# Attention steps of a hybrid decoder kernel: the second half of the keys' logits goes between the turnings of two groups of blocks

## The reference, cut to what matters

```python
score = jnp.where(causal[None], score, -jnp.inf)
_, idx = lax.top_k(score, topk)
...
logits = jnp.einsum('bthd,btkhd->bthk', qb, k_sel).astype(jnp.float32) * dh ** -0.5
logits = logits + jnp.moveaxis(bias, -1, -2)
logits = jnp.where(valid[:, :, None, :], logits, -jnp.inf)
p = jax.nn.softmax(logits, axis=-1).astype(v.dtype)
return jnp.einsum('bthk,btkhd->bthd', p, v_sel)
```

## Time and profile before

| | us |
|---|---|
| median of 3 runs | 990.1 |
| lowest and highest | 987.07 and 993.2 |
| the profiled execution's own time | 989.08 |
| its span, first to last instruction | 987.0 |
| PE busy | 947.3 |
| PE weight loads busy | 780.4 |
| DVE busy | 638.4 |
| ACT busy | 530.9 |
| POOL busy | 343.1 |

### The profile page before, as it was taken

The page is one execution under the profiler, slowest core; times in us unless marked ns, Lnnn a source line. Parts: engine busy times, 40 slices in busy tenths (PEclk is TensorE's granted clock), DMA queues, the critical chain, the costliest instruction groups (busy, mean ns, idle before and its releaser), DMA issues.

```text
span 987.0 us, 15061 instructions
## 1 busy us (share of the span) xinstructions
PE 947.3 (96%) x5650; PEld 780.4 (79%) x5650; DVE 638.4 (65%) x1101; ACT 530.9 (54%) x909; POOL 343.1 (35%) x437
## 2 busy tenths in 40 slices
PE   7999999899998999899998889999999999999997
PEld 5888899888776777677776768888888888888885
DVE  5348899599698935546464716673668492989252
ACT  6647688867664345546464744343364453785211
POOL 0022265466776535342322642201322221225100
PEclk9999999999999999999999989999999999999999
DMA  9515321001332342330112452221311121113062
GB/s 350 164 44 76 54 64 44 2 23 53 97 97 64 98 128 66 129 97 22 40 48 97 172 191 86 85 105 56 96 44 43 44 64 43 43 43 129 1 213 85
DMA packets 70014, 83.88 MB, mean 85 GB/s; under 512 B 3448, under 2 KB 52664, under 8 KB 69944
## 3 DMA queue, kind: packets, MB, share of 16 engines
q1 hardware_dynamic: 68528, 81.33, 25.7%
q10 hardware_dynamic: 1416, 1.63, 1.5%
HBM read 64.07 MB, written 18.35 MB: 84 GB/s over the span
## 4 chain that ended last, share of the span: by engine, by line
PE 55%; DVE 5%; ACT 3%; issue 2%; DMA 2%; POOL 1%; DVEq 0%; POOLq 0%; ACTq 0%
PE ps L1758 16%; PE ps L1760 16%; PE ps L1759 16%; PE ps L2013 2%; PE ps L2029 2%; DVE prob L1526 1%; PE ps L1870 1%; DMA g_two<-gla_d 1%; POOL g_two L785 1%; DMA gla_d<-g_two 1%; PE ps L2094 1%; DVE tmp L1627 1%; ACT pT L1118 0%; POOL score L797 0%; PE ps L1872 0%
## 5 line engine op out<-in xcount | busy, mean ns | idle before, releaser
L1758 PE MATMUL ps<-hH,wH 128*128 128x512 f32 (+1 forms) x356 | 138.7, 390 | 1.0 <-DVE scaled L1508 0.9
L1760 PE MATMUL ps<-hH,wL 128*128 128x512 f32 (+1 forms) x356 | 135.6, 381 | 0.0
L1759 PE MATMUL ps<-hL,wH 128*128 128x512 f32 (+1 forms) x356 | 135.3, 380 | 0.0
L1758 PE MATMUL ps<-h1H,w_slot_H 128*128 128x512 f32 x256 | 99.8, 390 | 0.0
L1760 PE MATMUL ps<-h1H,w_slot_L 128*128 128x512 f32 x256 | 99.6, 389 | 0.0
L1759 PE MATMUL ps<-h1L,w_slot_H 128*128 128x512 f32 x256 | 99.6, 389 | 0.0
L1371 DVE TENSOR_SCALAR_CACHE_REDUCE junk<-score,cand 128x768 bf16<-128x768 f32 (+3 forms) x128 | 96.7, 810 | 1.1
L681 POOL TENSOR_TENSOR wL<-raw,wH 128x1024 fp32r<-128x1024 f32 x28 | 70.3, 2517 | 57.0 <-ACT wH L873 56.5
L678 POOL TENSOR_TENSOR w_slot_L<-raw,w_slot_H 128x1024 fp32r<-128x1024 f32 x16 | 40.7, 2547 | 125.6 <-ACT w_slot_H L869 125.6
L1758 PE MATMUL ps<-wH,hH 128*128 128x256 f32 x256 | 75.2, 294 | 3.7 <-ACT bv L957 3.0
L1758 PEld LDWEIGHTS ps<-hH,wH 128*128 128x128 f32 x356 | 67.0, 188 | 14.5 <-issue 2.0
(11 more groups left out here) (288 smaller groups left out, 2347.5 us busy)
## 6 DMA issues: line engine op xcount, KB each, us to landing
raw<-in_even_w_in SPq DMA_DIRECT2D x28, 512.0 KB, 4.1
raw<-in_odd_w_in SPq DMA_DIRECT2D x16, 512.0 KB, 3.9
xt<-in_x_cols SPq DMA_DIRECT2D x8, 512.0 KB, 9.2
xn<-in_x SPq DMA_DIRECT2D x8, 512.0 KB, 10.0
gate_d<-gst SPq DMA_DIRECT2D x16, 256.0 KB, 2.1
raw_row<-in_even_w_out SPq DMA_DIRECT2D x8, 512.0 KB, 3.4
xt<-in_x SPq DMA_DIRECT2D x8, 512.0 KB, 3.5
x_d<-xt SPq DMA_DIRECT2D x8, 512.0 KB, 2.6
```

Of the source, the lines that this page charges most:

```text
L1758: pe.matmul(dst, lH, rH, start=k == 0, stop=False)
L1759: pe.matmul(dst, lH, rL, start=False, stop=False)
L1760: return pe.matmul(dst, lL, rH, start=False, stop=k == nk - 1)
```

## The change

`head_product` and `head_logits` get an argument that says which of the two banks to fill. In a step that has no filling, whose predecessor has two groups of blocks to turn, and whose own logits take two banks, PE now fills the first bank of both heads, turns the first group of step a - 1, fills the second bank of both heads, and then turns the second group. The wait for `s_masked` stands ahead of the first half, and `s_full` is raised after the second. These are steps 6, 7, 14, 15, 22, 23, 29, 30 and 31, nine of 32; the others are as before. No matmul, copy or DMA is added or removed.

```diff
--- before.py
+++ after.py
@@ -1860,12 +1860,12 @@
 
         pe.wait_ge(ik_twice, 32)
 
-        def head_product(e, b, w, q, k):
+        def head_product(e, b, w, q, k, only=range(2)):
 
             rows = slice(64 * e, 64 * e + 64)
             (qh, ql), (kh, kl) = [t[rows] for t in q], [t[rows] for t in k]
             banks, wb = pieces(w)
-            for i in range(banks):
+            for i in range(only[0], min(banks, only[-1] + 1)):
                 cols = slice(i * wb, (i + 1) * wb)
                 yield pe.matmul(ps[:, b + i, 0:wb], qh, kh[:, cols], start=True, stop=False)
                 yield pe.matmul(ps[:, b + i, 0:wb], qh, kl[:, cols], start=False, stop=False)
@@ -1989,18 +1989,20 @@
             if part == 3:
                 last.then_inc(proj_full, 1)
 
-        def head_logits(n):
+        def head_logits(n, banks=range(2)):
             p, qb = divmod(n, NT)
             toks = slice(qb * P, (qb + 1) * P)
             h, l = qkH[p % 2], qkL[p % 2]
-            pe.wait_ge(proj_free, low_count("pair", p, 1 if qb < NT // 2 else 3))
-            if n:
-                for e in range(2):
-                    pe.wait_ge(s_masked[e], n)
-            both = side_by_side([head_product(e, S_BANK[e], keys(qb), (h[:, 0, toks], l[:, 0, toks]), (h[:, 1, :], l[:, 1, :]))
+            if 0 in banks:
+                pe.wait_ge(proj_free, low_count("pair", p, 1 if qb < NT // 2 else 3))
+                if n:
+                    for e in range(2):
+                        pe.wait_ge(s_masked[e], n)
+            both = side_by_side([head_product(e, S_BANK[e], keys(qb), (h[:, 0, toks], l[:, 0, toks]), (h[:, 1, :], l[:, 1, :]), banks)
                                  for e in range(2)])
-            for e, ins in enumerate(both):
-                ins.then_inc(s_full[e], 1)
+            if banks[-1] >= pieces(keys(qb))[0] - 1:
+                for e, ins in enumerate(both):
+                    ins.then_inc(s_full[e], 1)
 
         def turn(g):
             n, first, m = BLOCKS[g]
@@ -2051,11 +2053,14 @@
         for a in range(NW + 2):
             parts = filler(a)
             groups = blocks_of[a - 1] if 1 <= a <= NW else []
+            halved = a < NW and not parts and len(groups) == 2 and pieces(keys(a % NT))[0] == 2
             if a < NW:
-                head_logits(a)
+                head_logits(a, range(1) if halved else range(2))
             for i, g in enumerate(groups):
                 turn(g)
                 if i == 0:
+                    if halved:
+                        head_logits(a, range(1, 2))
                     while parts:
                         pair_part(*parts.pop(0))
             if groups:
```

## The result

The changed kernel takes 991.24 us in the median of 22 runs (989.27 to 997.33), the kernel before 988.77 us in as many (985.96 to 993.9). The ratio is 1.0033, with an interval of 1.0021 to 1.0044: 3.3 us slower, 2.1 to 4.4. (The ratio has an estimate of its own; the two medians, taken by themselves, are 2.5 us apart.) That is within 1% and in the direction of the forecast; the forecast step was +1.7 us, half of it.

A forecast was written before the change was run, and what follows sets the result against it. PE, busy for 96% of the span, was taken to bound the kernel wherever it then works without a gap. Terms 0 + 1.9 - 0.2 = +1.7 us took the median from 990.1 to 991.8 us, range 988.0 to 996.0.

The forecast's parts named there:

- The place: Steps 14, 15, 22 and 23: the loop through the engines pays in these two pairs, +0.5 to +3.5 us, chance 0.64.
- The wait inside the first turnings: Head 1's first-group turnings need step a - 1's exponent, forecast to be just there in time; costed at nothing.
- The price of a halved step: Logits complete 1.08 us later in each halved step: 0.87 for eight turnings and 0.21 for the extra round trip.
- my strongest reading: Each switch between logits and turnings waits out the row before: 0.4 us a round trip, sum about 1 us higher.
- Steps 14 and 15: Late logits delay step 15's masking by 1.2 us and head 1's exponent by 0.95; with 22 and 23, +1.9 us.
- the slack: Step 15: head 1's exponent waits for ACT, busy with head 0, so 0.26 of the 1.2 us lateness is absorbed.
- Steps 6 and 7: Delay covered by DVE's late start in 6 and POOL's scaling in 7; no change, otherwise 1 us.
- Steps 29 to 31: Head 1's masking follows a gating after both groups' turnings; step 29 gains, the two others nothing: -0.2 us.
- B: Rival: PE's wait between the turnings sets a step; nine steps gain 0.25 us each, -2.2 us; chance 0.2.
- C: Rival: the loop pays everywhere, 1.1 us in each of nine steps, +9.9 us at most; chance 0.13.

The follow-up runs named there:

- the fastest kernel: Kernel before the change with POOL's third and fourth scaling one step later and a filling part moved from steps 5, 13, 21 to 6, 14, 22: 983.66 us, ratio 0.9944.

## Why the prediction was right, and where a term was too small

**The place.** Right. All of the loss in the traces lies in steps 14 and 15 and 22 and 23, at the mechanism named: the last logit matmul behind eight turnings, DVE waiting for it, and the filling behind the exponent of head 1.

**The wait inside the first turnings.** Costed at nothing, and in step 15 of the change head 0's and head 1's turnings are one row of eight with no idle before it. Right.

**The price of a halved step, 1.08 us.** Too small: the logits of 512 keys took 1.66 us from the first start to the last end, and now 2.90 (461.29 to 463.80 and 0.39), 1.24 more. I had the turnings' 0.87 right and the switching at 0.21. It is 0.37. I took one switch from the first logit pair's longer row and one from the last pair's, both of which show. Missing was the way from the last turning to the next logits: eight turnings occupy PE for 1.02 us here (462.20 to 463.22) and for 0.87 in the earlier trace rows, where a full-array matmul follows. No row of before has logits right behind turnings. The Trainium skill's rule on draining at a mode change, which I had weighed against the rows (TensorEngine Tiling (Array Packing), Key Properties), would by my strongest reading have given 0.4 a round trip; the traces agree with that size, 0.37, and I had chosen the smaller. They do not show the form that I gave it: the first half's last pair is followed by the turnings after 0.37 us (461.83 to 462.20), not after its whole row of 0.44.

**Steps 14 and 15, +0.95 us each pair.** Measured +1.35. Of the 0.4 between, about 0.16 is the switching in step 15 and 0.2 the lateness that step 14 leaves, 0.3 where I had 0.1: 0.15 of this again the switching (the logits take 1.23 us more, 1.08 forecast), 0.02 their length (1.47 us, not 1.45), and the rest DVE's start 0.04 us behind the last of them. About 0.05 is left for the slack, of which the run with steps 15 and 23 shows 0.21 (1.25 late in step 15, 1.04 in step 16) instead of 0.26. Two pairs: 2.7 instead of 1.9.

**Steps 6 and 7, nothing.** Right, and for the reason given; with POOL's scaling out of step 7 the same halving costs 0.98 us, where I had said 1.

**Steps 29 to 31, -0.2 us.** Right in size, by the traces. From the logits of 29 to the split of the first mixed tile it is 26.28 us before, 26.10 with the full change and 26.07 with only these steps halved; nine of the ten traces in which they are not halved lie between 26.28 and 26.30 (the tenth, 26.39, is the one with the low clock at step 29). What makes -0.13 and -0.40 of it in the table lies ahead of the logits of 29: ACT waited 0.93 and 0.69 us for its output weights, 0.88 before. Such waits, once with the low clock behind them, move that column by up to 2.7 us in other executions, and a timing cannot tell 0.2 us. The reason, a gain in step 29 alone, is roughly so: with these steps halved the time from the logits to `turn_gla` falls by 0.52 us in step 29 and 0.16 in step 30, but 0.32 us of new wait stands ahead of the logits of 30.

**The sum.** +1.7 forecast, +2.6 in the traces at the end of attention, +3.3 (2.1 to 4.4) by the ratio and +2.5 between the medians. The term that was mis-sized is the switching, 0.37 us where the forecast had 0.21, which then counted in four steps. The difference between 2.6 and 3.3 lies inside the interval and need not have a cause.

**The rivals.** B, the wait between the turnings, had its gain in PE's rows and nowhere in the time. C needed the cover in steps 6 and 7 to be gone, and it was there; nor did the near bias and the gating of steps 29 to 31 queue behind the late masking.

## What to carry to other kernels

When PE waits at two places of a step, ask which of them the loop through the other engines ends. Work put into a gap is free only if nothing that the loop waits for stands behind it; here the last logit matmul did, and some 0.4 us of PE's (the wait of 0.25, and 0.88 instead of 1.04 for the row behind it) were bought with logits complete 1.24 us later. In this kernel the idle time was worth having, but by moving what held up the loop (POOL's queue) and then putting in work that nobody waits for.

## What the runs showed of the hardware that I had not expected

**A round trip between half-array and full-array matmuls costs PE 0.37 us**: 0.08 in the first pair of logits, 0.14 in the last (461.83 to 462.20, less 0.23), and 0.15 by which eight turnings that logits follow occupy it longer (1.02 instead of 0.87). It does not grow with the number of turnings: with one head's four between the halves the logits of step 15 were complete 0.78 us later than before, with eight 1.24, so four more cost 0.46 and some 0.3 is fixed. Not all of it belongs to the change between the two kinds. Before the change, filling that follows turnings, both on the full array, also begins with a product that occupies 0.31 us where the next takes 0.23, while turnings behind filling cost nothing more:

```profile
450.48 0.48 PE L1758 MATMUL ps<-hH,wH 128*128 128x512 f32 x1
450.79 0.39 PE L1759 MATMUL ps<-hL,wH 128*128 128x512 f32 x1
...
453.08 0.39 PE L1760 MATMUL ps<-hH,wL 128*128 128x512 f32 x1
453.31 0.38 PE L2013 MATMUL ps<-ident,prob 128*128 128x128 f32 x2
```

That leaves 0.29 us where half the array and the whole meet. What PE does in it no run here shows.

**The granted clock falls in some executions and not in others, and this is larger than what was studied.** PE had waited 3.33 us (filling moved) and 2.01 us (15 and 23 halved) before the logits of 8 where the clock was 0.57 over 4 us, costing 1.2 us each time; after 1.69 and 1.84 us, before the change and with it, it did not fall. The Trainium skill, TensorE: Matmul & The Clock Gate, "What's actually happening", says that an idle TensorE has half the clock, and the traces agree: both levels occur and the fall comes behind a wait. But the length of the one wait does not decide it. The first mixed tile ends the same wait of 3.29 us in all the traces, and behind it the granted clock over 575 to 600 us has a mean of 0.86, 0.93 or 0.94 in most of them and 1.00 in two (15 and 23 halved; filling moved, scaling later). In the 22 runs of the changed kernel the mean clock is between 0.989 and 0.997, and the higher it is, the shorter the time (correlation -0.84), by 0.9 us for each 0.001; in 61 runs of the kernel before it is 0.5 us (correlation -0.69). The six runs of the fastest kernel have a mean of 0.9962 and those of before in the same series 0.9944; so some of its 5.5 us, of which the trace explains 3.2, may be that PE's shorter waits let the clock fall less often. By the two slopes this would be 0.9 to 1.6 us, an estimate. One trace for each kernel cannot show how often it falls, and this stays open.
